# One input load becomes four, and the parameter rows change queue and turn

## The reference

```python
def first_block(x, ...):      # depth 1
    h = x
    h = h + 0.5 * swiglu_ffn(rmsnorm(h, ffn1_norm), ffn1_w_in, ffn1_w_out)   # 1024 -> 2 x 2816 -> 1024
    u = rmsnorm(h, mix_norm) @ w_mix_in
    h = h + concat(short_conv_mixer(u...), gated_deltanet_mixer(u...)) @ w_mix_out
    h = h + 0.5 * swiglu_ffn(rmsnorm(h, ffn2_norm), ffn2_w_in, ffn2_w_out)
    return rmsnorm(h, final_norm)

def second_block(x, mem, ...):   # depth 2: a gated linear attention layer, then a sparse attention layer
    ...                          # each with an attention over mem and a convolved FFN
    return rmsnorm(h, final_norm_2)
```

## Time and profile before

| | us |
|---|---|
| median of 3 runs | 2781.93 |
| lowest, highest | 2776.48, 2791.48 |
| the profiled execution | 2777.02 |
| its span, first to last instruction | 2775.3 |
| TensorE busy | 2520.8 (91%) |
| VectorE busy | 1312.3 (47%) |
| ScalarE busy | 943.4 (34%) |

### The profile page before, as it was taken

How to read it: one execution, slowest core, us unless ns; L and a number is a source line. 1 busy time by engine, 2 the same in 40 slices (tenths; PEclk the granted TensorE clock), 3 DMA queues, 4 the chain that set the end, 5 groups by cost and what they waited for, 6 DMA issues and landing times.

```text
span 2775.3 us, 32393 instructions
## 1 busy us (share of the span) xinstructions
PE 2520.8 (91%) x12244; PEld 2010.2 (72%) x12244; DVE 1312.3 (47%) x2028; ACT 943.4 (34%) x1448; POOL 150.1 (5%) x132
## 2 busy tenths in 40 slices
PE   8999999948799999999867999999799888899996
PEld 6888868727678888867664478878687656688885
DVE  4334343466444434343372266653343674566633
ACT  4222241362333222243222143342322663433322
POOL 2000010004010000020000100000101000100001
PEclk9999999958999999999968999999899899999998
DMA  4333223300023332222100233322555101233321
GB/s 133 98 91 99 98 77 96 94 0 1 19 80 95 95 91 99 91 77 65 27 0 23 76 91 98 96 93 92 113 108 161 41 28 46 76 98 96 94 98 46
DMA packets 321901, 215.19 MB, mean 78 GB/s; under 512 B 40938, under 2 KB 306685, under 8 KB 321801
## 3 DMA queue, kind: packets, MB, share of 16 engines
q1 hardware_dynamic: 318536, 199.88, 25.1%
q0 software_dynamic: 3264, 13.94, 1.5%
HBM read 211.65 MB, written 8.44 MB: 79 GB/s over the span
## 4 chain that ended last, share of the span: by engine, by line
PE 82%; DVE 8%; ACT 6%; issue 2%; POOL 1%; DMA 1%; POOLq 0%; ACTq 0%; DVEq 0%
PE bank L499 16%; PE bank L500 16%; PE bank L501 16%; PE bank L613 6%; PE bank L612 6%; PE bank L611 6%; PE bank L483 3%; PE bank L786 2%; POOL rstd L732 1%; ACT arena L2216 1%; PE bank L2049 1%; PE bank L1720 1%; DVE arena L2142 1%; PE bank L1259 1%; PE bank L1273 1%
## 5 line engine op out<-in xcount | busy, mean ns | idle before, releaser
L499 PE MATMUL bank<-xH,wH 128*128 128x512 f32 (+2 forms) x2056 | 814.6, 396 | 67.8 <-DVE xL L685 19.6
L501 PE MATMUL bank<-xH,wL 128*128 128x512 f32 (+2 forms) x2056 | 807.4, 393 | 0.0
L500 PE MATMUL bank<-xL,wH 128*128 128x512 f32 (+2 forms) x2056 | 807.3, 393 | 0.0
L376 ACT ACTIVATE wH<-raw 128x1024 fp32r<-128x1024 f32 (+2 forms) x355 | 368.8, 1039 | 978.4 <-PE bank L501 505.6
L404 DVE TENSOR_TENSOR wL<-raw,wH 128x1024 fp32r<-128x1024 f32 (+2 forms) x355 | 431.5, 1216 | 565.0 <-ACT wH L376 564.7
L499 PEld LDWEIGHTS bank<-xH,wH 128*128 128x128 f32 (+2 forms) x2056 | 384.8, 187 | 169.2 <-issue 46.2
L500 PEld LDWEIGHTS bank<-xL,wH 128*128 128x128 f32 (+2 forms) x2056 | 385.3, 187 | 87.6 <-issue 1.7
L501 PEld LDWEIGHTS bank<-xH,wL 128*128 128x128 f32 (+2 forms) x2056 | 384.6, 187 | 88.3
L613 PE MATMUL bank<-g_hi,wL 128*128 128x512 f32 x704 | 280.0, 398 | 0.0
L611 PE MATMUL bank<-g_hi,wH 128*128 128x512 f32 x704 | 277.5, 394 | 1.2 <-DVE wL L404 1.2
L612 PE MATMUL bank<-g_lo,wH 128*128 128x512 f32 x704 | 277.1, 394 | 0.0
(11 more groups left out here) (302 smaller groups left out, 2520.1 us busy)
## 6 DMA issues: line engine op xcount, KB each, us to landing
raw<-in_ffn_w_in SPq DMA_DIRECT2D x88, 512.0 KB, 3.8
raw<-in_w_up SPq DMA_DIRECT2D x88, 512.0 KB, 3.8
raw<-in_ffn_w_out SPq DMA_DIRECT2D x44, 512.0 KB, 3.2
raw<-in_w_down SPq DMA_DIRECT2D x44, 512.0 KB, 3.3
raw<-in_w_mix_in SPq DMA_DIRECT2D x28, 512.0 KB, 3.9
raw<-in_gla_w_in SPq DMA_DIRECT2D x16, 384.0 KB, 3.4
raw<-in_w_kv_shared SPq DMA_DIRECT2D x12, 512.0 KB, 6.1
rel_wide<-rel_rows POOLq DMA_DIRECT2D x12, 512.0 KB, 12.3
```

Source lines behind the costliest of these rows:

```text
L376: nc.scalar.activation(wH[:, half_slot(s, i, j), 0:n], raw[:, k, 0:n], ACT.Copy).then_inc(sem("w_hi"), 1)
L499: pe.matmul(o, wh, xa, start=a, stop=False)
L500: pe.matmul(o, wh, xb, start=False, stop=False)
L501: last = pe.matmul(o, wl, xa, start=False, stop=z)
```

## The change

x is loaded in four DMAs, one for each block of 128 tokens, each with a semaphore of its own. The 20 parameter DMAs go to ScalarE's queue, at the head of its list. TensorE turns the parameters first, waits until they are copied to `par`, and then turns x block by block: for each t, as soon as its block has landed, all eight tiles k, tile k into bank k. A tile is reported as turned in the last block only. VectorE copies the parameters and makes `gain4` before its four copies of `hT`. SyncE loads the panels of `ffn0_up` right behind x, and the nine small loads come after them.

```diff
-        def load_sp(sp):
+        def params_in(act):
...
-                    sp.dma_start(stage[row:row + k, tile, :], flat[at:at + k]).then_inc(sem("par_staged"), 16)
+                    act.dma_start(stage[row:row + k, tile, :], flat[at:at + k]).then_inc(sem("par_staged"), 16)
...
         def load_pe(pe):
             pe.wait_ge(sem("const"), NCONST)
-            pe.wait_ge(sem("x_landed"), 16)
-            for k in range(KD):
-                if k >= 4:
-                    pe.wait_ge(sem("h_act" if k % 2 == 0 else "h_dve"), (k - 4) // 2 + 1)
-                for t in range(TT):
-                    last = turn(pe, bank[4 + k % 4][:, t * P:(t + 1) * P], rows[:, t, k * P:(k + 1) * P])
-                last.then_inc(sem("x_turned"), 1)
             pe.wait_ge(sem("par_staged"), 16 * NPAR_DMA)
             for t in range(NPT):
                 k = min(P, NPAR - t * P)
                 last = turn(pe, bank[t // 4][:, t % 4 * P:t % 4 * P + k], stage[0:k, t, :], k)
             last.then_inc(sem("par_turned"), 1)
-            pe.wait_ge(sem("h_dve"), KD // 2)
+            for t in range(TT):
+                pe.wait_ge(sem(f"x_landed{t}"), 16)
+                if t == 0:
+                    pe.wait_ge(sem("par"), -(-NPT // 4))
+                for k in range(KD):
+                    last = turn(pe, bank[k][:, t * P:(t + 1) * P], rows[:, t, k * P:(k + 1) * P])
+                    if t == TT - 1:
+                        last.then_inc(sem("x_turned"), 1)
 
         def load_act(act):
+            params_in(act)
             act.sem_inc(sem("evac_act"), CREDIT_EV)
             for k in range(0, KD, 2):
                 act.wait_ge(sem("x_turned"), k + 1)
-                nc.scalar.activation(hT[:, k, :], bank[4 + k % 4][:], ACT.Copy).then_inc(sem("h_act"), 1)
+                nc.scalar.activation(hT[:, k, :], bank[k][:], ACT.Copy).then_inc(sem("h_act"), 1)
 
         def load_dve(dve):
...
-            for k in range(1, KD, 2):
-                dve.wait_ge(sem("x_turned"), k + 1)
-                nc.vector.tensor_copy(hT[:, k, :], bank[4 + k % 4][:]).then_inc(sem("h_dve"), 1)
             dve.wait_ge(sem("par_turned"), 1)
...
               .then_inc(sem("gain4"), 1)
+            for k in range(1, KD, 2):
+                dve.wait_ge(sem("x_turned"), k + 1)
+                nc.vector.tensor_copy(hT[:, k, :], bank[k][:]).then_inc(sem("h_dve"), 1)
...
         def _(sp):
-            sp.dma_start(rows[:, :, :], A["x"][0].rearrange("(t p) c -> p t c", p=P)).then_inc(sem("x_landed"), 16)
-            load_sp(sp)
+            for t in range(TT):
+                sp.dma_start(rows[:, t, :], A["x"][0, t * P:(t + 1) * P, :]).then_inc(sem(f"x_landed{t}"), 16)
+            load_panels(sp, "ffn0_up")
...
-            for s in plan.order:
+            for s in plan.order[1:]:
                 load_panels(sp, s.name)
```

## The result

| | before | changed |
|---|---|---|
| median, 20 runs each, us | 2781.32 | 2786.98 |
| lowest, highest | 2776.24, 2792.17 | 2783.09, 2796.52 |
| ratio, 95% interval | | 1.0024 [1.0014, 1.0034] |
| the profiled execution | 2777.02 | 2787.45 |
| its span | 2775.3 | 2785.7 |

The changed kernel is 5.7 us (0.2%) slower by the medians and 10.4 us by the two profiled spans. The ratio of the table is not the quotient of the medians: 1.0024 is 6.7 us, its interval 3.9 to 9.5 us. A second set (12 runs against 23) gave 2793.49 against 2781.46, ratio 1.0037 [1.0022, 1.0053].

The account below looks back on a forecast made before the run. TensorE was taken as the bound, behind an opening chain to the first dense matmul at 20.09 us. Parameters landing at 12 plus 13.4 gave 25.4, 5.3 us later; forecast 2785 us, between 2782.3 and 2787.2, range 2774 to 2796.

Parts of the forecast that it names:

- TensorE is the only limit behind the opening: After the first dense matmul at 20.09 us: no further TensorE wait to 300 us, so its shift moves the end equally.
- M: Start of the first dense matmul, at 20.09 us before the change; forecast at 25.4 us, 5.3 us later.
- Splitting x hides nothing: Opening: all four x blocks land before the first is turned at 14.3 us; price three more SyncE issues of 0.46 us.
- T + 13.4: Opening: first dense matmul 13.4 us (12.9 to 13.9) after the last parameter row lands: 2.3 + 5.1 + 2.4 + 3.64.
- T = 12: Landing of the last parameter row from ScalarE's queue, forecast at 12 us, bounds 10.0 and 15.7, with 1 us for sharing.
- rival B: Opening: parameters starve beside x and panels, landing at 15.7 us or later; +9 to +12 us, 2795; chance 10%.
- The estimate by engine counts: Parameter DMAs: odd-row pieces use few engines, so parameters land near 13.8 us, first matmul 1.8 us later than forecast.
- Early panels cost nothing but T: SyncE issues first panels at about 2.7 us, not 12.33: no gain, their cost counted in the parameters' landing time.
- the small loads are covered: Nine small loads behind first-stage panels: 3.8 us in a 3.7 us gap, 0.1 us spills against 19.5 us of cover.
- rival C: First dense matmuls: the slow-clock stretch doubles from 4.1 to 8.2 us, +2.05 us, 2787; chance 8%.
- x lands at 8.5 to 9.5: Opening: x ends at 8.5 to 9.5 us, its 2 MB sharing with 0.26 MB, well before its turns at 14.3.
- Rival A: Opening: parameters land early and blocks are turned as they land; at best 5.0 us earlier, 2775; chance 7%.

Follow-up runs that it names:

- x_one: Changed kernel with x loaded as one DMA again; first dense matmul at 30.05 us against 30.09, span 2785.2 us.
- panels_wait_timed: The changed kernel with first panels held until all parameters landed, repeated without edit and timed: median 2782.01 us against 2777.40 before, ratio 1.0015.
- panels_wait: Changed kernel, but SyncE issues the first panels only after all parameter rows have landed; first dense matmul at 24.56 us, span 2789.0 us.
- x_first: Changed kernel with TensorE turning x blocks as they land and parameters after them, VectorE's copies likewise; first dense matmul at 23.10 us, span 2779.1 us.
- two_queues_wait: Against changed: x turned first, parameter DMAs divided between ScalarE and SyncE, panels held until parameters landed; median 2778.09 us, ratio 0.9998 to before.

## Why the prediction was right or wrong

The forecast of 2785 within 2774 to 2796, and slower by less than 0.5%, held: 2786.98. That it came within 2 us is luck: the shift in it, 5.3 us, was half of the 10.0 that the opening shows. The median of before lay 4.3 us above its profiled execution and that of the changed kernel 0.5 below its own, a draw of the runs that takes 4.8 off the 10.4 between the spans. Its parts:

- **TensorE is the only limit behind the opening, so M moves the end.** Right: M + 10.00, span + 10.4, no new wait of TensorE up to 300 us.
- **Splitting x hides nothing.** Right (x_one).
- **T + 13.4.** Right: 13.49, and 12.3 to 13.5 in all executions with this order, where the range said 12.9 to 13.9. By terms: to the x turns 2.36 (2.3 forecast), 24 turns and the 25th 5.58 to 5.60 (5.1 taken, 5.6 the slow end), the copies 2.07 (2.4), from the first xH to the matmul 3.46 (3.64). In this execution the clock did not rise early: 25 slow turns, the upper end of my term. That is again a draw: in panels_wait_timed, with the same turns, the pace doubled 3.0 us after the first x turn, and M - T was 12.28, under the range.
- **T = 12.** This is the term that was mis-sized: 16.60, beyond even my upper bound of 15.7. It is rival B, which I had given one chance in ten. Two parts of it failed. The base without competition was put at 11, from the shape of a tail, where the same rows had landed at 12.89 in the very trace of before and land at 11.85 from ScalarE's queue (panels_wait). And 1 us was put for sharing where it was 4.75 (panels_wait). Of the 4.75, 1.1 is slower issue, which ended at 9.36 and in panels_wait at 8.28 (forecast: 7.9); the rest is landing. The rows did not come in a little late and ahead of the panels but among them: the four panels landed at 11.7, 13.9, 17.2 and 18.7, the rows at 16.60, after the second and before the third. My upper bound was too low as well, since these panels ended 3 us after its 15.7. The estimate by engine counts, T of 13.8, which I wrote down and did not use, was nearer and still 2.8 short: the shape of the pieces costs 2.1 us without panels and 2.5 beside them, so it explains little of what the panels add.
- **So the shift of 5.3 us was too small by half**: 10.0 by the profiles. That the medians show 5.7 is no confirmation of 5.3; the second set shows 12.0.
- **Early panels cost nothing but T; the small loads are covered.** The second is right: the first down panel was issued 10.68 us later than before and not 10.26, so 0.4 us spilled and not 0.1, and none was paid. "Nothing but T" was taken as a small matter, and T was 3.7 us later than before and 4.6 later than forecast.
- **The first matmuls run slow as long as before** (rival C not taken): 4.87 us against 4.11, 0.4 us of loss.
- **x lands at 8.5 to 9.5**: the last block landed at 9.98, a little late, and still 9 us before the first turn of x.
- **Rival A (faster)**: T never came near 6.7. The best of all was 11.8. What would have made the split of x pay is the other order on TensorE, x_first, together with an early T.

Undone one by one from the changed kernel: without the panels beside the parameters M is 5.5 and 6.0 us earlier (4.75 and 4.8 of it T, the rest a clock that rose sooner); with x turned first it is 7.0 earlier, M - T 7.7 smaller; the block order is 1.2 of these 7.7 (an estimate), the x turns standing behind the parameters the rest. The terms overlap, so they don't add up to 10.0.

## What to carry to other kernels

A small load that gates everything should not share its time with bulk loads on another queue: on one queue, ahead of the bulk, these rows landed at 12.9; on a second queue beside the bulk at 16 to 18.8. Put what needs a late input last on an in-order engine, and what has already landed first. And before a shift of 0.2% is read from medians, look whether the executions of one kernel differ among themselves by more, and compare the landmark in the trace.

## What was not expected of the hardware

- The issue of the same 20 DMAs took 0.357 us each on SyncE and 0.37 to 0.47 on ScalarE (0.37 and 0.38 in the two executions with the panels held back, 0.40 to 0.47 in the six with panels beside them).
- The same 256 small matmuls took 14.56 or 25.10 us, with the granted clock at 1.00 or 0.56.
- The turns ran at the slow pace of 0.214 us each and later at the fast one with the granted column at 1.00 throughout, before the change and after; the pace, not that column, tells the clock in the opening. In every trace here the record behind the column begins only about where the pace first doubles (14.2 us before the change, 24.7 after it), and ahead of it the column prints 1.00.
- A semaphore's last increments can come 2.3 us after the last data packet (two_queues_wait), 0.174 us apart, where the kernels with the rows on one queue show 0.5 to 0.7 us from the last data packet to the full count.
